# The last tile of a residual stage: its square and sum ahead of the next weight split, and where the modulation lots stand

## The reference, cut to what matters

```
def rms_norm_2(x, g):
    xf = x.astype(jnp.float32)
    y = xf * lax.rsqrt(jnp.mean(xf * xf, axis=-1, keepdims=True) + EPS)
    return (y * g.astype(jnp.float32)).astype(x.dtype)

def modulate(h, shift, scale):
    return h * (1.0 + scale) + shift
...
        x = x + 0.5 * mx[2] * swiglu_2(modulate(rms_norm_2(x, norm_g[layer, 0]), mx[0], mx[1]),
                                     ffn_w_in[layer, 0], ffn_w_out[layer, 0])
```

## Time and profile before

| what | us |
|---|---|
| median of 3 runs | 2931.82 (2931.29 to 2933.14) |
| the profiled execution, its own time | 2933.65 |
| its span, first to last instruction | 2931.8 |
| PE busy in it | 2774.6 |
| DVE busy | 1635.0 |
| ACT busy | 1133.5 |
| mean granted clock of TensorE | 0.965 of full speed |

### The profile page before, as it was taken

How to read it: one execution, slowest core, us unless ns; L and a number is a source line. 1 busy time by engine, 2 the same in 40 slices (tenths; PEclk the granted TensorE clock), 3 DMA queues, 4 the chain that set the end, 5 groups by cost and what they waited for, 6 DMA issues and landing times.

```text
span 2931.8 us, 39437 instructions
## 1 busy us (share of the span) xinstructions
PE 2774.6 (95%) x16254; PEld 2413.4 (82%) x16254; DVE 1635.0 (56%) x2663; ACT 1133.5 (39%) x1743; POOL 0.3 (0%) x5
## 2 busy tenths in 40 slices
PE   7999899999998998999989998999989999899898
PEld 6988899988898996888864786888868888688898
DVE  6653677656447776555551356555565444655654
ACT  6453444445434443223232343222232232344443
POOL 0000000000000000000000000000000000000000
PEclk9997999999899998999989999999999999999999
DMA  5532557544235774444431013444434444320554
GB/s 182 176 118 75 170 183 228 185 139 144 94 108 190 228 223 130 150 148 145 145 108 50 22 66 114 139 149 151 144 110 142 151 146 148 115 66 30 174 183 133
DMA packets 114050, 403.17 MB, mean 138 GB/s; under 512 B 12368, under 2 KB 15568, under 8 KB 113744
## 3 DMA queue, kind: packets, MB, share of 16 engines
q1 hardware_dynamic: 113872, 400.66, 42.3%
HBM read 399.56 MB, written 1.05 MB: 137 GB/s over the span
## 4 chain that ended last, share of the span: by engine, by line
PE 91%; DVE 4%; ACT 3%; issue 2%; DMA 0%; SPq 0%; DVEq 0%; ACTq 0%
PE psum L533 25%; PE psum L534 25%; PE psum L535 25%; PE psum L834 2%; PE psum L861 1%; PE psum L961 1%; PE psum L969 1%; PE psum L801 1%; PE psum L803 1%; ACT whi L1039 1%; PE psum L802 1%; ACT L1067 1%; DVE wlo L1417 1%; PE psum L529 0%; PE psum L927 0%
## 5 line engine op out<-in xcount | busy, mean ns | idle before, releaser
L533 PE MATMUL psum<-HHI,whi 128*128 128x256 f32 (+1 forms) x3456 | 1124.9, 325 | 57.5 <-DVE HLO L1483 32.4
L534 PE MATMUL psum<-HLO,whi 128*128 128x256 f32 (+1 forms) x3456 | 1115.7, 323 | 0.0
L535 PE MATMUL psum<-HHI,wlo 128*128 128x256 f32 (+1 forms) x3456 | 1114.9, 323 | 0.0
L1417 DVE TENSOR_TENSOR wlo<-wring,whi 128x1024 fp32r<-128x1024 f32 x590 | 707.9, 1222 | 410.3 <-ACT whi L1039 408.0
L1039 ACT ACTIVATE whi<-wring 128x1024 fp32r<-128x1024 f32 x590 | 607.0, 1053 | 465.8 <-PE psum L535 445.5
L533 PEld LDWEIGHTS psum<-HHI,whi 128*128 128x128 f32 x3456 | 667.9, 193 | 122.2 <-issue 64.3
L534 PEld LDWEIGHTS psum<-HLO,whi 128*128 128x128 f32 x3456 | 667.8, 193 | 48.9 <-issue 1.4
L535 PEld LDWEIGHTS psum<-HHI,wlo 128*128 128x128 f32 x3456 | 667.1, 193 | 48.3
L533 PE MATMUL psum<-HIDHI,whi 128*128 128x256 f32 (+1 forms) x1056 | 357.2, 338 | 0.0
L534 PE MATMUL psum<-HIDLO,whi 128*128 128x256 f32 (+1 forms) x1056 | 357.2, 338 | 0.0
L535 PE MATMUL psum<-HIDHI,wlo 128*128 128x256 f32 (+1 forms) x1056 | 357.1, 338 | 0.0
(11 more groups left out here) (280 smaller groups left out, 2125.0 us busy)
## 6 DMA issues: line engine op xcount, KB each, us to landing
wring<-ffn_in SPq DMA_DIRECT2D x264, 512.0 KB, 4.2
wring<-mod_w SPq DMA_DIRECT2D x144, 512.0 KB, 4.3
wring<-ffn_out SPq DMA_DIRECT2D x96, 448.0 KB, 3.5
wring<-w_proj SPq DMA_DIRECT2D x66, 512.0 KB, 4.2
wring<-w_gate SPq DMA_DIRECT2D x64, 512.0 KB, 3.7
wring<-ffn_out SPq DMA_DIRECT2D x48, 512.0 KB, 4.2
wring<-w_up SPq DMA_DIRECT2D x20, 512.0 KB, 3.3
wring<-w_out SPq DMA_DIRECT2D x16, 512.0 KB, 3.3
```

Of the source, the lines that this page charges most:

```text
L533: mm(out_, w[0], a[0], start=start, stop=False)
L534: mm(out_, w[0], a[1], start=False, stop=False)
L535: return mm(out_, w[1], a[0], start=False, stop=stop)
L1417: TTN(wlo[:, i, :], wring[:, raw_slot(tag, k), :], whi[:, i, :].bitcast(F32), ALU.subtract).then_inc(sem("weights_lo"), 1)
```

## The change

Two edits. First, in `residual` and `ffn`, on ACT and on DVE: at the last tile of a stage the split of the lot ahead no longer stands between the tile's add and its square and sum, but behind the loop. Second, the table of modulation lots: none stands behind lots 0 to 3 of a stage's first product (0 to 4 for most), so none is worked together with the lot that is split at the last tile. `ffi` carries 10 and not 11, `ffi2` 20 and not 22 (the last one 1 and not 4), `down` 3 and not 4 (behind 5, 6, 7), `qkv` 4 as before (behind 5, 7, 9, 11 and not 1, 3, 5, 7), and each `ffo2` of the three that carry any 16 and not 12: behind two of the three lots of a tile. The total stays 144.

```diff
-    def spread(tag, lots_, step):
+    def spread(tag, lots_):
+
         nonlocal n
-        for k in range(step - 1, lots_, step):
+        for k in lots_:
             if n < DEPTH * MOD_T:
...
-        spread(f"ffi{l}", 2 * FT, 4)
-        spread(f"ffo{l}", 3 * KT, 6)
+        spread(f"ffi{l}", range(7, 2 * FT, 4))
+        spread(f"ffo{l}", range(5, 3 * KT, 6))
     for l in range(DEPTH):
-        spread(f"ffi2{l}0", 2 * FT, 2)
-        spread(f"ffo2{l}0", 3 * KT, 2)
-        spread("down" if l == 0 else "qkv", 8, 2)
-        spread(f"ffi2{l}1", 2 * FT, 2 if l == 0 else 4)
+        spread(f"ffi2{l}0", range(5, 2 * FT, 2))
+        spread(f"ffo2{l}0", [k for k in range(3 * KT) if k % 3])
+        spread("down" if l == 0 else "qkv", range(5, 8) if l == 0 else range(5, 12, 2))
+        spread(f"ffi2{l}1", range(5, 2 * FT, 2 if l == 0 else 4))
         if l == 0:
-            spread(f"ffo2{l}1", 3 * KT, 2)
+            spread(f"ffo2{l}1", [k for k in range(3 * KT) if k % 3])
...
                 for k in range(KT):
-                    split_ahead(tag, k)
+                    if k < KT - 1:
+                        split_ahead(tag, k)
                     act.wait_ge(*done("x_ready", (tag, k)))
                     square(norm, n, k)
+                split_ahead(tag, KT - 1)
...
                     add_tile(k, bank_of((tag, k)), (tag, k), coef, n, (tag, k), l)
-                    split_ahead(tag, k)
+                    if k < KT - 1:
+                        split_ahead(tag, k)
                     add_square(norm, n, k)
+                split_ahead(tag, KT - 1)
```

More of the change, by code:

```diff
@@ L1081, in ffn @@
                 for k in range(3 * KT):
-                    split_ahead(tag_out, k)
+                    if k < 3 * KT - 1:
+                        split_ahead(tag_out, k)
                     if k % 3 == 2:
@@ L1085, in ffn @@
                         square(norm, norm_n, k // 3)
+                split_ahead(tag_out, 3 * KT - 1)
             def project(l):
```

## The result

The changed kernel takes **2903.11 us** (median of 4 runs, 2902.98 to 2904.47), the kernel before in the same comparison 2931.56 (4 runs, 2930.67 to 2933.14). The ratio is 0.9903 with a 95% interval of 0.9891 to 0.9915: 28.45 us less, between 1.09% and 0.85%. The forecast was 2901 with a range of 2895 to 2908.

The account below looks back on a forecast made before the run. TensorE bounds the kernel, losing time at stage boundaries waiting for DVE's running sum. Idle time 26.3 plus matmul of ones 4.3 gave 30.6 us off 2933.65, 2903.05; less 1.83 for the median, 2901 us, range 2895 to 2908.

Parts of the forecast that it names:

- The idle time, 26.3 us: TensorE's wait before the norm sums at nine boundaries shrinks by 26.3 us; the last boundary doesn't change.
- the built 2.44: New idle time before a 512-column sum, put together from add, square and hand-overs: 2.44 us instead of 5.39.
- The matmul of ones, 4.3 us: The norm sums' matmuls run more at full clock: 1.39 us saved at 256 columns, 2.9 at 512, together 4.3.
- Three quarters: Share taken of the 3.9 us that full clock would save on 512-column sums: 2.9 us, bounds 0 and 3.9.
- The split behind the sum, nothing: At boundaries the late split is covered on ACT (0.25 us spare) and DVE (1.3) at 256 columns: costs nothing.
- The modulation lots, nothing: Their new places in `ffo2`, `down` and `qkv` cost nothing; `qkv` has 7 us of cover for 2.4 to 4.4.
- 2 to 3 us either way: Spread from nine restarts at half clock, each moving independently by up to 1.4 us.
- From the profiled execution to the median: Last step: runs' median taken 1.83 us below the profiled execution's time, turning 2903.05 into 2901 us.
- (a): Rival: the late split is not covered, ACT's copy waits for a late load, some 12 us lost: 2913; chance 0.06.
- (c): Rival: denser modulation lots in `ffo2` outrun the 4 raw slots, TensorE stops inside the stage: 2973 us; chance 0.02.
- (d): Rival: the change doesn't reach the path, something other than the sum is late: some 2925 us; chance 0.02.
- (b): Rival: the clock stays up through whole boundaries, nine restarts at full clock, 18 us more gained: 2883; chance 0.04.

Follow-up runs that it names:

- the best kernel: Changed kernel plus unwanted matmuls behind every norm sum but the last, in first-block attention and before `uq`; `qkv` modulation lots and keys' rotation later: 2876.97 us.
- the order alone: Changed kernel with the old table of modulation lots, so only square and sum ahead of the split at the last tile: 2906.48 us.
- the experiment with DVE alone: Changed kernel with ACT's loops put back to the order of before, so that only DVE splits late: 2907.0 us.
- with fillers: Changed kernel plus matmuls that compute nothing wanted behind each `norm_sum` but the last, 3 at 256 columns, 4 at 512: 2883.23 us.
- a front filler: The best kernel plus one unwanted 512-column matmul between a stage's last product and its `norm_sum`: 2878.94 us.

## Why the prediction was right, point by point

**The idle time, 26.3 us: right.** Measured 26.4 from the rows above, 26.5 in the waits. At 256 columns 1.51 to 1.65 against 1.64 taken from the last boundary; at 512 columns 2.45 and 2.52 against the built 2.44; at the first with 512 columns 1.99 against 1.97. To take the last boundary, which had the new order already, as the model of the others was worth more than any sum of durations, and the one built from rows agreed because each hand-over in it was read too.

**The matmul of ones, 4.3 us: under-sized.** It gave 5.6. All nine ran at full clock, and the 512-column pair takes 1.10 and not 1.15. Three quarters had been taken for a clock that falls at 2.0 us of idle time in one row and is up for part of a sum after 4.24; here it was up at 2.52. The rule of the Trainium skill, "TensorE: Matmul & The Clock Gate", section "Why this matters for your kernels", by which short gaps keep the clock, would have given 5.3 and was nearer for this kernel. The runs don't bear it out in general: after the same 2.45 us the sum took 1.94 us in the best kernel, and 2.05 in the one with the order alone.

**The split behind the sum, nothing: right.** 1.06 us of cover on ACT and 2.39 on DVE at 512 columns, in the rows above; the gap behind the sum didn't grow. At the thinnest place, ACT at 256 columns, 0.36 us were left where the prediction had 0.25. At the nine together the gap even shrank by 0.66 us, which no step had foreseen (3.81 at 256 columns, 5.58 at most of 512). That both engines have to give way, ACT too, the experiment with DVE alone shows: 3.9 us.

**The modulation lots, nothing: right.** The waits show none of TensorE inside the three `ffo2` with the denser lots. In `qkv` the cover shrank as worked out. DVE's last rotation, then ACT's copy of the values, which answer to the earlier trace rows:

```profile
2554.91 0.42 DVE L1647 TENSOR_TENSOR arena<-arena 128x256 f32<-128x256 f32 x1
```

```profile
2558.96 1.21 ACT L1304 ACTIVATE arena<-psum 128x256 f32<-128x256 f32 x4 [4.64 <-PE psum L536]
```

2558.96 - 2555.33 = 3.6 us are left of 7: later by 3.3, inside the 2.4 to 4.4.

**The clock elsewhere: not in the sum.** Boundaries together gave 32.6 us; 2.0 went back at the restarts. Two more places changed against each other. In `uq` TensorE stands 3.78 us in both kernels, and the clock was up behind it before and down after. PEclk in 2 us, before and after:

```profile
1557.00:1559.00 2.00, 2.00 (x6) 0.95 (x5) 1.36 (x2) 0.60 (x1) 0.00 (x0) 1.00 0.00 0
```

```profile
1539.00:1541.00 2.00, 2.00 (x3) 0.97 (x4) 0.95 (x2) 1.01 (x2) 0.00 (x0) 0.50 0.00 0
```

In `qkv`, behind a stall of 2.2 us in both, it was the other way round, in 4.4 us:

```profile
2560.70:2565.10 4.40, 4.39 (x24) 4.39 (x25) 4.33 (x8) 1.06 (x1) 0.00 (x0) 0.61 0.68 201
```

```profile
2535.60:2540.00 4.40, 4.37 (x36) 4.37 (x37) 4.33 (x8) 1.12 (x3) 0.00 (x0) 1.00 0.74 212
```

That is 2.6 us lost and 1.7 won. Behind the gaps of the attention in the first block another 0.4 was lost. These together leave 29.3 us, and the span became 30.6 shorter: 1.3 us are not attributed, 0.8 of them between the restart of `qkv` and the sum behind `swao`. The "2 to 3 us either way" that the prediction allowed for the clock was about right in size. Its reason, restarts that move independently by chance, is wrong: they repeat, and what one loses more or less the next ones partly take back.

**From the profiled execution to the median: the step that was off.** The profiled executions differ by 30.66 us, the sum was 30.6, and 2903.05 would have been the forecast without a correction; 2903.11 was measured. The 1.83 us taken off belonged to the one profiled execution of before, which was slower than its median (a second execution of it gave 2931.8 with 1.3 us less lost at the restarts); the changed kernel's stood at its median (2902.99 and 2903.11). That the sum met the profiled difference to 0.1 us is in part luck: what it left out cancelled (for it 1.3 more at the sums, 0.7 at the gaps behind them and the 1.3 not attributed; against it 2.0 at the restarts, 0.9 in `uq` and `qkv`, 0.4 in the attention).

**The rivals.** (a) a late load behind the split on ACT didn't occur, and neither did (c). (d) is excluded by the order alone, 25.5 us. (b), the clock up through the whole boundary, was not the change's doing; with fillers, which are another cause than shorter gaps, the kernel took 2883.23, where the prediction had put this case at 2883: nine restarts are worth the 18 us that it gave them, or a little more (20).

## What to carry to other kernels

At a boundary where the next stage waits for a reduction, nothing that isn't its input belongs between the last tile and its share of the reduction, on any engine in the chain; work for later goes directly behind it, as long as the wait that follows is longer. What two edits bring can overlap: each alone took the modulation products out of the way, so their single gains don't add. And where the idle time at the boundaries has been cut, the half clock behind it costs nearly as much: 22 us at nine restarts here, which matmuls without use in the gap bring back nearly whole.

## What the runs showed of the hardware that was not expected

- Time lost to the half clock at a restart repeats from run to run, within 0.05 us at seven of nine places in the changed kernel and at four in the one before, and a shift of 1 or 2 us in front of the second restart is forgotten by the fifth. The rise of the clock kept its distance to the rise before it (197.97 or 197.98 us in four executions) where the restart between them moved by up to 1.4 us.
- The length of a gap alone doesn't tell whether the clock stays: after 2.96 and 3.11 us it fell at three places of four, after 3.78 us it stayed up in one kernel, after 2.54 and 2.03 us it stayed in one and fell in another.
- Matmuls in a gap can keep the clock: with 1.24 to 1.39 us of idle time left at 256 columns and 2.15 to 2.23 at 512, nothing was lost at any of the nine restarts. It is no rule: with a front filler and the same gaps, two of the nine lost 1.7 us each.
- The clock also fell where TensorE had no gap at all. In the attention of each layer of the first block it was at half for 34.1 us on end (from 233.3 and from 776.0 us in the changed kernel, and alike in every kernel here), and TensorE was busy throughout. If that work would run twice as fast at full clock, up to 17 us are lost each time, together more than at the nine restarts. What sets it is open; many of the matmuls there have operands of 8 partitions only. The stretch in the changed kernel:

```profile
233.31:267.44 34.13, 34.13 (x100) 24.19 (x99) 4.34 (x8) 3.43 (x7) 0.00 (x0) 0.50 0.02 6
```
